# Splitting the weights of the mixing stages in quarter blocks at every tile

## What is computed

```python
for i in range(DEPTH):                      # 4 layers: fox, gla, gdn, fox
    y = rmsnorm(h, norm_mix[i])
    mix = ...                               # fox_mixer, gla_mixer or gdn_mixer
    h = h + mix
    h = h + swiglu(rmsnorm(h, norm_ffn[i]), w_gate_up[i], w_down[i])
```

## Time and profile before

| | |
|---|---|
| median of three executions | 2506.14 us (2498.27 to 2516.81) |
| the profiled execution | 2510.86 us |
| its span, first to last instruction | 2509.2 us |
| PE busy | 2314.7 us, 92% |
| DVE busy | 1565.8 us, 62% |
| ACT busy | 1213.0 us, 48% |
| POOL busy | 620.8 us, 25% |
| mean granted clock of PE | 0.967 of full |
| read from HBM | 339.38 MB, 136 GB/s over the span |

### The profile page before, as it was taken

One profiled execution on the slowest core, in us unless ns is written; L12 is line 12 of the kernel. 1 busy time (PEld: TensorE's weight loads), 2 busy tenths in 40 slices (PEclk: granted clock), 3 DMA queues, 4 the chain that ended last, 5 costly groups with the idle time before them and its releaser, 6 DMA issues. The chain is left out here.

```text
span 2509.2 us, 47433 instructions
## 1 busy us (share of the span) xinstructions
PE 2314.7 (92%) x19122; PEld 2192.1 (87%) x19122; DVE 1565.8 (62%) x2514; ACT 1213.0 (48%) x1861; POOL 620.8 (25%) x744
## 2 busy tenths in 40 slices
PE   4999999999999898899989999996899998899998
PEld 4878999889999787799988799996698998688998
DVE  4665655746655664565456666546567975656994
ACT  4555444545444642354345555443446554445553
POOL 3114211013111020121121142112174530053550
PEclk9999999999999898899999999998899999989999
DMA  4224545324545221155542345462253554233554
GB/s 162 102 85 135 174 158 190 133 84 152 170 163 170 85 67 54 53 174 177 157 134 97 102 145 174 157 217 79 76 184 128 184 172 164 68 118 131 188 169 133
DMA packets 52715, 342.94 MB, mean 137 GB/s; under 512 B 5888, under 2 KB 7104, under 8 KB 20160
## 3 DMA queue, kind: packets, MB, share of 16 engines
q1 hardware_dynamic: 51984, 336.26, 40.5%
q0 software_dynamic: 560, 4.26, 0.4%
HBM read 339.38 MB, written 1.05 MB: 136 GB/s over the span
## 5 line engine op out<-in xcount | busy, mean ns | idle before, releaser
L732 PE MATMUL ps<-arena_r,ring_hi 128*128 128x272 f32 (+1 forms) x6688 | 1604.5, 289 | 14.4 <-DVE arena L2119 7.4
L732 PEld LDWEIGHTS ps<-arena_r,ring_hi 128*128 128x128 f32 x6688 | 1177.0, 192 | 18.6 <-DVE arena L2119 7.8
L732 PE MATMUL ps<-y_r,ring_hi 128*128 128x272 f32 (+1 forms) x3424 | 1022.6, 299 | 49.6 <-DVE ring_lo L1993 23.0
L732 PE MATMUL ps<-y_r,ring_lo 128*128 128x272 f32 (+1 forms) x3424 | 987.8, 289 | 0.0
L1993 DVE TENSOR_TENSOR ring_lo<-ring,ring_hi 128x2048 fp32r<-128x2048 f32 (+1 forms) x348 | 738.2, 2122 | 385.1 <-ACT ring_hi L1459 384.5
L732 PEld LDWEIGHTS ps<-y_r,ring_hi 128*128 128x128 f32 x3424 | 658.9, 192 | 79.2 <-issue 40.4
L1459 ACT ACTIVATE ring_hi<-ring 128x2048 fp32r<-128x2048 f32 (+1 forms) x348 | 607.5, 1747 | 114.8 <-DMA ring<-dn 46.1
L732 PEld LDWEIGHTS ps<-y_r,ring_lo 128*128 128x128 f32 x3424 | 660.4, 193 | 0.0
L732 PE MATMUL ps<-arena_r,ring_lo 128*128 128x272 f32 (+1 forms) x1632 | 469.4, 288 | 0.0
L732 PEld LDWEIGHTS ps<-arena_r,ring_lo 128*128 128x128 f32 x1632 | 311.2, 191 | 0.0
L1459 ACT ACTIVATE arena<-arena 128x272 f32<-128x272 f32 (+7 forms) x199 | 93.4, 472 | 403.6 <-DVE arena L2552 268.8
(11 more groups left out here) (233 smaller groups left out, 1719.7 us busy)
## 6 DMA issues: line engine op xcount, KB each, us to landing
ring<-gu SPq DMA_DIRECT2D x88, 1024.0 KB, 5.1
ring<-dn SPq DMA_DIRECT2D x64, 704.0 KB, 4.0
ring<-up SPq DMA_DIRECT2D x44, 1024.0 KB, 5.1
ring<-fox_in SPq DMA_DIRECT2D x32, 1024.0 KB, 5.1
ring<-sdn SPq DMA_DIRECT2D x32, 704.0 KB, 4.0
ring<-gdn_in SPq DMA_DIRECT2D x16, 1024.0 KB, 5.0
ring<-in SPq DMA_DIRECT2D x16, 1024.0 KB, 5.1
ring<-gla_in SPq DMA_DIRECT2D x12, 1024.0 KB, 5.1
```

Source lines behind the costliest of these rows:

```text
L732: return nc.tensor.matmul(dst, w, mv, start=start, stop=stop)
```

## The change

In the stages whose splits are put in by `hooks`, a half block is split in two pieces of half its width (a quarter of the block each), on ACT and on DVE, and for blocks of four tiles one piece stands at every tile in place of one whole half at every second tile. For a block of eight tiles the pieces stand at every second tile. Blocks of fewer than four tiles, and the feed-forward stages, go on splitting whole halves. The semaphores count quarters: a piece raises `hi_ready` and `lo_ready` by one, a whole half by two, and the values waited for are doubled. PE waits for `lo_ready` twice per half block, at its start and in its middle, in all stages.

In numbers: 58 of the blocks, 116 half blocks, are split in quarters. Two new helpers, `share` and `quarters`, give the columns of a piece and the count after it.

```diff
--- before.py
+++ after.py
@@ -541,15 +541,28 @@
         def acc(tile, width, m=P, banks=BANKS):
             return ps[0:m, tile % banks, 0:width]
 
+        def share(g, part):
+
+            w = half_width[g]
+            return slice(0, w) if part is None else slice(part * w // 2, (part + 1) * w // 2)
+
+        def quarters(at, part):
+
+            return 2 * at + (2 if part is None else part + 1)
+
         def hooks(split, n, tpb):
 
             def at(t):
                 g = n.block + t // tpb + 1
                 if g < len(half_width):
-                    if t % tpb == 0:
-                        split(g, 0)
-                    if t % tpb == tpb // 2:
-                        split(g, 1)
+                    if tpb < 4:
+                        if t % tpb == 0:
+                            split(g, 0)
+                        if t % tpb == tpb // 2:
+                            split(g, 1)
+                    elif t % (tpb // 4) == 0:
+                        quarter = t % tpb // (tpb // 4)
+                        split(g, quarter // 2, part=quarter % 2)
             return at
 
         def flat(a):
@@ -746,11 +759,13 @@
                         for k in range(kc):
                             if t == 0 and first:
                                 ready(k)
-                            half, at = divmod((j * kc + k) * P, tpb * kc * P // 2)
+                            width_of_half = tpb * kc * P // 2
+                            half, at = divmod((j * kc + k) * P, width_of_half)
                             slot = (2 * (n.block + b) + half) % SLOTS
-                            if at == 0:
-
-                                pe.wait_ge(lo_ready, i * (2 * turn) + (2 * (n.block + b) + half + 1))
+                            for part in range(2):
+
+                                if 0 <= at + P - 1 - part * width_of_half // 2 < P:
+                                    pe.wait_ge(lo_ready, i * (4 * turn) + quarters(2 * (n.block + b) + half, part))
                             hi, lo = ring_hi[:, slot, at:at + P], ring_lo[:, slot, at:at + P]
                             shi, slo = src(k)
                             dst = acc(n.tile + t, width, P, banks)
@@ -1462,12 +1477,12 @@
 
                 nc.scalar.preload_act_table_set("natural_log_exp_and_others")
 
-            def split(g, half, i=0):
+            def split(g, half, i=0, part=None):
 
                 at = 2 * g + half
-                slot, w = at % SLOTS, half_width[g]
+                slot, cols = at % SLOTS, share(g, part)
                 act.wait_ge(loaded[slot], i * 16 + 16 * (at // SLOTS + 1))
-                fn(ring_hi[:, slot, 0:w], ring[:, slot, 0:w], ACT.Copy).then_inc(hi_ready, 1)
+                fn(ring_hi[:, slot, cols], ring[:, slot, cols], ACT.Copy).then_inc(hi_ready, 2 if part is None else 1)
 
             def norm_x(src, gain, width, base, before=None, last=False, first=False):
 
@@ -1985,13 +2000,13 @@
                 mark(ins)
                 v.wait_ge(dve_step, steps[0])
 
-            def split(g, half, i=0):
+            def split(g, half, i=0, part=None):
 
                 at = 2 * g + half
-                slot, w = at % SLOTS, half_width[g]
-                v.wait_ge(hi_ready, i * 4 + (at + 1))
-                V.tensor_tensor(ring_lo[:, slot, 0:w], ring[:, slot, 0:w], ring_hi[:, slot, 0:w].bitcast(F32),
-                                ALU.subtract).then_inc(lo_ready, 1)
+                slot, cols = at % SLOTS, share(g, part)
+                v.wait_ge(hi_ready, i * 8 + quarters(at, part))
+                V.tensor_tensor(ring_lo[:, slot, cols], ring[:, slot, cols], ring_hi[:, slot, cols].bitcast(F32),
+                                ALU.subtract).then_inc(lo_ready, 2 if part is None else 1)
 
             def take(t, width, m=P):
 
```

## The result

The changed kernel takes 2523.98 us (median of 6 executions, 2519.32 to 2529.65), the kernel before 2505.6 (6 executions beside them). The ratio is 1.0063, 95% interval 1.0044 to 1.0082: slower by 0.6%, some 16 us. I had forecast no change, 2505. The time lies above the 2490 to 2521 that I gave the forecast by itself, and near the upper end of the 2484 to 2527 that reached to the rivals; the direction was not forecast.

The account below looks back on a forecast made before the run. PE, 92% busy, bounds the kernel; only its idle time in six mixing stages, 125.7 us, can give. gdn +10, fox -7, gla and hybrid -4.5 sum to -1.5: 2505 us, range 2490 to 2521, to the rivals 2484 to 2527.

Parts of the forecast that it names:

- What bounds the kernel: Whole program: PE busy 92%; only the six mixing stages have idle PE to give, 125.7 us; no weight is late.
- the cost of the instructions: All quartered blocks: two pieces cost 0.18 us more on ACT, 0.16 on DVE; PE's added waits taken as 0.
- gdn up to tile 11, "say +10": gdn tiles 2 to 11: the added DVE-ACT-DVE round trip in odd tiles lengthens the stretch, 10.6, say +10 us.
- gdn from tile 12, "-0.4": gdn's later tiles: shorter PE waits, -9.3 us, nearly cancelled by new waits in odd tiles; sum -0.4.
- the clock, "5 us either way": Whole program: more and shorter PE waits can shift time at the low clock level by 5 us either way.
- fox, "-3.5 each": Both fox stages: shorter start, waits for normalised heads traded evenly, last tiles giving 0.8; -3.5 us each, -7 together.
- my -2.7: Start of each fox stage: shorter splits ahead of the first normalised head and the forget sums give -2.7 us.
- Hybrid and gla, "-4.5": gla and both hybrid stages: shorter splits before PE's waits, added pieces in dense DVE stretches; together -4.5 us, bounds -9, +4.
- My -1.5 and -2.2 for the hybrid stages: First hybrid stage -1.5 us, DVE also being slow there for another reason; hybrid stage at 2097 -2.2 us.
- The sum: Whole program: gdn +10, fox -7, gla and hybrid -4.5 make -1.5 us, say 2505; chance 0.70.
- (a): Six mixing stages: halving helps everywhere, alternate pieces fall into slack; -63 us, 2443, or 2475 in half strength; chance 0.14.
- (b): gdn tiles 2 to 31 and dense hybrid stretches: ACT round trips added, nothing given back; +31 us, 2537; chance 0.16.

Follow-up runs that it names:

- the waits alone: Kernel before with every half split whole and where it was, plus only PE's second wait per half block and doubled counts: 2515.69 us, 1.0020.
- the late kernel: Changed kernel with quarter pieces at every tile, but DVE subtracting each piece one tile after ACT made it: 2469.90 us, 0.9818.

## Why the prediction was wrong

**What bounds the kernel; the cost of the instructions.** Right. A 1024-wide piece takes 1.045 and 1.26 us, a 512-wide one 0.62 and 0.69; PE's wait for low parts is still only at the start, 23.1 of 23.6 us. The gate-and-up stages moved by 0.3. (The intervals of their matmuls scatter between 120 and 129 ns, not by the 20 ns from which I had bounded the price of a wait.)

**gdn up to tile 11, "say +10".** The mechanism was right, and so was its size: the plain pair takes 10.05 us where I had 10.2, the sums of tile 5 come 5.4 us later where I had 4.8, and DVE reaches the roots of tile 11 10.4 us later. The stretch is 12.5 longer because PE, after waiting 5.94 us for these roots, makes its next 54 matmuls at the low clock. That wait and its clock were not in the term.

**gdn from tile 12, "-0.4", and the clock, "5 us either way".** This is the step that failed. What I had added up there, the waits, came out about even: PE's idle time is the same to 2 us, and the shorter waits for L2401 (4.2 for 8.0) are paid by the new ones that I had named: 4.8 us behind the query roots of tile 19, 0.9 before, where I had put 2.9 more, and 2.9 for the keys of tile 25, 0.2 before, where I had put 2.6 more. But I let the clock into no term and gave it no sign, and it was one-sided: a mean of 0.9635 over ten executions for 0.967, 7 us of the 16 to 19. Its largest place is this stretch, 38 to 61 us at the low level in place of 23 to 39, which took 8 us more by the mean of the eight profiles and 1.7 more by the two pairs of the kernels compared.

**fox, "-3.5 each".** The second term that failed. Over four profiles with quarters and six with whole halves: fox 0 183.3 against 185.5, fox 1 181.6 against 183.5, -2.2 and -1.9; less 0.45 per low us, -2.2 and -0.4. The seven waits for L2106 came as I said. The shorter start, my -2.7, did not: in fox 1 the second tile starts 8.1 us into the stage in the changed kernel and 11.1 in the profile of rows 2, but 8.1 in the second profile of the kernel before too, and 7.9 to 8.1 in the four others with whole halves there. The 11.1 is a tile into which ACT comes late, after 3.69 us of waiting for a load of the ring, and which runs 3.4 us at the low clock. DVE does come earlier to the bias of the forget gates, but waits there for POOL, as told below.

**Hybrid and gla, "-4.5".** Better than forecast: hybrid stages -4.4 and -4.2, their short stages -1.2 and -0.2, gla -1.4, by the same profiles. In all -11. My -1.5 and -2.2 for the hybrid stages were about half or less of what they gave; by which waits was not looked at.

**The sum.** I had +10 - 7 - 4.5 = -1.5. Measured by stages, quarters against whole halves: gdn +20.5 by its two parts, fox -4, hybrid and gla -11, the stages between them, which I had put at nothing, +4: +9. (The changed kernel's two profiles against the two of the kernel before give gdn +14 and a whole of +8.5 and +12.9.) The kernels with quarters in gdn only and everywhere but in gdn say much the same: +22 and -16 against the waits alone, +6, and those waits 0 to 5 more. The ratios of the whole say +16 and +19. Each of these ratios is uncertain by some 5 us, which can close most of the gap; I can't place the rest.

**Rivals.** (a) had its own mechanism refuted, since DVE's waits in gdn grew; that halving alone can help is nevertheless true, by the two pieces at even tiles (-0.7%, where I had expected no clear change). The sentence of the Trainium skill ("Perfetto Trace Analysis", on optimizing Scalar/DVE operations), that breaking up instructions may let work complete sooner, holds here with the place as its condition: the same pieces cost 0.6% one by one, and give 0.7% in pairs and 1.8% one tile late. (b) was nearer: a loss through the round trip in gdn. But its price after tile 11, 12 us for more waiting of PE, did not come in PE's idle time; what came, 8 by the mean of the profiles, came by the clock.

## What to carry to other kernels

Where one engine's output is another's input within the same step, ask how long ago the first was begun before asking how large a piece is: a piece whose input was made a tile earlier did no harm in any tile of the mixing stages here, and a piece whose input is only now being made cost its whole round trip in each tile of the stretch that DVE and ACT paced. So smaller pieces in more places multiply the hand-over, unless the consumer is moved one step behind. And a sum of waits is not the whole price of a change on a kernel that is bound by PE: give the time at its low clock a term of its own, signed, by what a us at the low level cost in the profile (0.45 here), and compare kernels that are closer than 1% by several executions and their mean clocks, not by one profile of each.

## What the hardware showed that I had not expected

**DVE's small TENSOR_SCALAR and POOL's memset.** At the start of fox DVE adds a bias to 16 rows (L2080, now L2095). By shape, in the kernel before and in the changed one:

```profile
L2080 DVE TENSOR_SCALAR arena<-arena,par 16x272 f32<-16x272 f32 x2 | 1.2, 610 | 0.1
```
```profile
L2095 DVE TENSOR_SCALAR arena<-arena,par 16x272 f32<-16x272 f32 x2 | 3.3, 1661 | 0.1
```

It went from 0.61 to 1.66 us with the same operands (0.48 and 1.50 in the second pair of profiles, 3.0 in the late kernel). The timeline of fox 1 in the changed kernel shows what it ran beside, POOL first:

```profile
1294.31 3.73 POOL L2792 MEMSET arena<- 2x4352 f32 x1
...
1296.26 1.93 DVE L2095 TENSOR_SCALAR arena<-arena,par 16x272 f32<-16x272 f32 x1
```

The memset ends at 1298.04 and the TENSOR_SCALAR at 1298.19. Before, the memset ended at 1289.72 and the TENSOR_SCALAR at 1289.87, but had begun only at 1289.26. DVE's other instructions beside the memset keep their durations (the evacuation 0.43). Over both fox stages of all 18 profiles it is the same: where the instruction begins before the memset has ended, 30 times of 36, it ends 0.15 us behind it, and takes 0.57 to 3.04 us; in the other six it takes 0.35. So where DVE comes to it earlier, it waits there for POOL instead. In fox 1 it comes at 9.84 us into the stage in the changed kernel and at 11.17 in the second profile of the kernel before, and ends at 11.8 in both: the 1.3 us are lost. It takes 1.05 longer on average over the two stages. The Trainium skill ("SBUF — State Buffer", "Who interferes with whom") says that DVE and GpSimd share a pair of ports, that `tensor_scalar` can take it (in its two-port modes) and fully blocks while a GpSimd instruction holds it. The rows agree; that the port is the cause was not tried by itself.

**A small DMA behind a large one.** In fox 1 PE waits for the rows that POOL's DMA writes after the forget sums: 3.2 us before, 4.7 in the changed kernel, with the same 17 KB. It took 3.8 us to land before and 5.4 after, beside a ring load of 1 MB that took 5.7 and 7.4. In the profiles of other kernels the same wait is between 2.9 and 5.0, whole halves among them, so this is where the transfer happens to fall, not a law of the change.

**The clock.** Stages with the same instructions differ from one profile to another by up to 8 us (fox 1: 180.4 to 188.4 with whole halves, at mean clocks of 0.97 and 0.93). gdn's second part has the same idle time of PE in both programs and up to twice the time at the low clock. In gdn most of the low stretches begin in a longer wait of PE, one in the wait of 5.94 us ahead of tile 12 in all four profiles with quarters there, one in the 3 us wait for the keys of tile 25 in all four with quarters in that part; but how long such a stretch lasts differs between executions, 10 to 31 us for the latter. What decides that I have not found; it stays open.
